# Attention tasks handled in pairs, one pair of sums on another engine, and a new order at the mixer's entry, in one encoder layer on one Trainium2 core

## The chip, the cores and the metric

The program runs on one core of one Trainium2 chip. A core has TensorE (PE, the matrix engine; PEld is its loading of weights), VectorE (DVE), ScalarE (ACT), GpSimd (POOL) and SyncE (SP), each with a queue of its own that it works off in order, and semaphores between them. The metric is the device time of one execution in microseconds, as the median of three runs.

## What is computed

One layer of a streaming encoder for 512 prompt tokens and 32 sample tokens (T = 544), D = 1024, everything in float32:

```
r += 0.5 * post_ffn1(SwiGLU_1(pre_ffn1(r)))             # up1 and down1, D_FF = 2816
z  = pre_mix(r) @ w_in                                   # q | k | v | b | c | xv
     heads A: 8 query heads, 2 key/value heads; a query chunk of 64 sees its own chunk and the two before it;
              a learned sink logit in each softmax's denominator
     heads B: b * causal_depthwise_conv3(c * xv)
r += post_mix(concat(norm_A(A), norm_B(B)) @ w_out)
r += 0.5 * post_ffn2(SwiGLU_2(pre_ffn2(r)))             # up2 and down2
r += post_ple(sigmoid(pre_ple(r) @ w_ple_gate) * (p @ w_ple_proj))
```

All norms are RMS norms over the features. The layer also returns the newest keys, values and convolution rows.

## The kernel before

Activations lie with features on the partitions and tokens along the row; the 544 tokens are two halves of 272, A and B. Each float32 operand of a large product is split into a high part (ScalarE, a copy with rounding, "hi") and a low part (VectorE, the difference, "lo"), and a product is three matmuls: high by high, high by low, low by high. A *unit* is one 128 x 272 result in one of four PSUM banks (`bank`); unit n uses bank n mod 4, so PE may start a unit only when the result four units before it has been read out (*evacuated*). The other four PSUM banks are `misc`.

**Start.** PE turns (transposes) the tokens' tiles `x_tok` into `misc` and `bank`; ACT and DVE copy them to `r`, split the first weights and inputs, and PE begins the units of up1, each as a pass over the high parts (L1846, `hi_pass`) and one over the low ones (L1854, `lo_pass`).

**up1, up2.** After ten single units come seventeen *jobs* (`jobs`, `seven`): a 2x2 block product by seven products of 12 matmuls (Strassen's scheme), L1924 to L1927. A job needs sums of weight blocks: `first_sums` (DVE, L1310) makes two of them in `s31`; `weight_sums` (POOL, L659 and L661) makes two more in `s24`, the second from the first; then ACT makes the high parts (`block_hi`, L774) and DVE the low ones (`block_lo`, L1316) in four pieces per job, in `even_blocks` or `odd_blocks`. ACT copies partial results out of the banks (`kept`, L782 to L796), and DVE adds them. The first job's parts are made while PE is busy with single units, the second job's while it is busy with the first.

**Mixer entry.** down1's last results give two sums of squares over half B: one to scale `y_down`'s half B, one for `r`'s half A (its inverse, `rpre` A, scales the first units' results). PE adds the squares over the partitions (`all_sums`, L1819), ACT takes the root, DVE the inverse (`invert`, L1224). `chain_r` on DVE then updates the residual half B in eight steps (L1232 scale, L1239 add), and the places after single steps at which the units 0 to 3 (k, v, q0, q1 of half A) are evacuated are given in its table. PE needs those evacuations and ACT's high parts of the new residual for units 4 to 7.

**Mixer.** 36 units (`MIX_UNITS`, v = 0 to 35), and 17 attention *tasks* (16 of 64 queries by two heads' groups, one for the sample). Behind unit v = 10 + d PE does the scores of task d (`scores`, L2059), the transposes of task d-1's probabilities (`turn_probs`, L2005) and the weighing of the values for task d-2 (`weigh`, L2084 to L2093); ACT does the exponentials and copies the transposed probabilities, DVE the maxima, the scaling and the copying of the outputs. I call the block of these small matmuls behind a unit a *visit*. DVE's loop over v evacuates unit v, then takes the maxima of task d, then the low parts of a weight (`split_lo`), the output of task d-2 and the scaling of task d. The last rows of the convolution are turned on PE behind unit 33 (`conv_rows`).

The order on every engine is that of the code; nothing is planned at run time.

## Time and profile before

| | |
|---|---|
| median of three runs | 1059.75 us (1059.62 to 1059.94) |
| the profiled execution | 1059.61 us, of which its span 1057.8 us |
| PE busy | 1034.4 us, 98% of the span |
| DVE, ACT, POOL busy | 697.1, 511.3, 277.0 us |
| mean granted TensorE clock | 0.995 |

Busy time of PE is that of pipelined matmuls: one lasts 0.29 us by its record, and in a full stream one starts every 0.12 to 0.125 us. What PE loses is therefore read from the distance between the starts of its instructions, and from the idle times that the profile puts down to a releaser. Times of a row are in microseconds from the span's start.

### The profile page before, as it was taken

The page shows a single profiled execution, that of the slowest core. Times are in us where ns is not written, and L with a number is a line of the kernel's source. Part 1 is how long each engine was busy: PE and PEld are TensorE (multiplying, and loading weights), DVE is VectorE, ACT ScalarE, POOL GpSimd, SP SyncE. Part 2 cuts the span into 40 slices and gives each one's busy share as a digit, 9 for nine tenths or more (in the row PEclk, how much of TensorE's full clock was granted, in tenths as well). Part 3 has the DMA queues.
Part 4 walks back from the last instruction along what each step waited for, and adds up shares of the span by engine and source line. Part 5 has one row for each costly group of instructions (what it writes and reads, how often), then busy time and mean ns, then how long its engine had stood idle before and what let it go on. Part 6 is the DMA issues. An engine that isn't in the chain of part 4 may idle for free.

```text
span 1057.8 us, 20089 instructions
## 1 busy us (share of the span) xinstructions
PE 1034.4 (98%) x8095; PEld 1014.5 (96%) x8095; DVE 697.1 (66%) x1051; ACT 511.3 (48%) x925; POOL 277.0 (26%) x212
## 2 busy tenths in 40 slices
PE   7999999999999999999999999999999999999997
PEld 6999999999999998888999999999999999999897
DVE  5889777777512269677695898987777741127843
ACT  5555555555522354434455555555555642126664
POOL 3114443431111142000323201443434011114221
PEclk8999999999999999999999999999999999999999
DMA  8214343435323303230234121442423532332102
GB/s 246 83 41 111 93 117 84 117 82 143 106 81 110 79 7 80 80 87 21 73 109 120 41 80 41 121 120 81 121 80 108 138 112 73 90 100 84 39 1 85
DMA packets 182678, 94.76 MB, mean 90 GB/s; under 512 B 11768, under 2 KB 180928, under 8 KB 182592
## 3 DMA queue, kind: packets, MB, share of 16 engines
q1 hardware_dynamic: 182576, 93.56, 32.0%
q8 instruction: 60, 0.98, 0.4%
q14 instruction: 26, 0.21, 0.1%
q10 hardware_dynamic: 16, 0.00, 0.0%
HBM read 91.15 MB, written 2.50 MB: 89 GB/s over the span
## 4 chain that ended last, share of the span: by engine, by line
PE 85%; DVE 9%; POOL 2%; ACT 2%; issue 1%; DMA 1%; SPq 0%; POOLq 0%; DVEq 0%; ACTq 0%
PE bank L1797 14%; PE bank L1799 14%; PE bank L1798 14%; PE bank L1924 9%; PE bank L1927 9%; PE bank L1926 9%; PE bank L1846 6%; PE bank L1854 2%; PE misc L2005 2%; PE misc L1924 1%; PE misc L1927 1%; PE misc L1926 1%; DVE w_split L1218 1%; DVE x_lo L1248 1%; DMA raw_up<-w_ffn_gate_up 1%
## 5 line engine op out<-in xcount | busy, mean ns | idle before, releaser
L1799 PE MATMUL bank<-h_hi,w_split 128*128 128x272 f32 x704 | 204.0, 290 | 0.0
L1797 PE MATMUL bank<-h_hi,w_split 128*128 128x272 f32 x704 | 203.0, 288 | 0.0
L1798 PE MATMUL bank<-h_lo,w_split 128*128 128x272 f32 x704 | 202.2, 287 | 0.0
L1218 DVE TENSOR_TENSOR w_split<-raw,w_split 128x1408 fp32r<-128x1408 f32 (+2 forms) x66 | 98.7, 1507 | 146.4 <-ACT w_split L714 146.4
L629 POOL TENSOR_TENSOR ssq<-ssq,sq 128x272 f32<-128x272 f32 x99 | 96.5, 975 | 221.6 <-ACT sq L719 216.1
L1798 PEld LDWEIGHTS bank<-h_lo,w_split 128*128 128x128 f32 x704 | 132.6, 188 | 0.1
L1797 PEld LDWEIGHTS bank<-h_hi,w_split 128*128 128x128 f32 x704 | 132.4, 188 | 0.1
L1799 PEld LDWEIGHTS bank<-h_hi,w_split 128*128 128x128 f32 x704 | 132.3, 188 | 0.0
L1924 PE MATMUL bank<-t_hi,even_blocks 128*128 128x272 f32 x432 | 125.3, 290 | 0.2
L1927 PE MATMUL bank<-t_hi,even_blocks 128*128 128x272 f32 x432 | 125.0, 289 | 0.0
L1926 PE MATMUL bank<-t_lo,even_blocks 128*128 128x272 f32 x432 | 124.4, 288 | 0.0
L659 POOL TENSOR_TENSOR s_rest<-s,raw_up 128x512 f32<-128x512 f32 x32 | 70.6, 2206 | 199.6 <-DVE s L1310 199.6
L714 ACT ACTIVATE w_split<-raw 128x1408 fp32r<-128x1408 f32 (+2 forms) x66 | 81.1, 1240 | 83.0 <-PE bank L1799 76.6
L1924 PE MATMUL bank<-t_hi,odd_blocks 128*128 128x272 f32 x384 | 111.5, 290 | 2.0 <-ACT kept L789 1.1
L1927 PE MATMUL bank<-t_hi,odd_blocks 128*128 128x272 f32 x384 | 111.1, 289 | 0.0
L1926 PE MATMUL bank<-t_lo,odd_blocks 128*128 128x272 f32 x384 | 110.5, 288 | 0.0
L1798 PE MATMUL bank<-x_lo,w_split 128*128 128x272 f32 x320 | 92.1, 288 | 0.0
L1924 PEld LDWEIGHTS bank<-t_hi,even_blocks 128*128 128x128 f32 x432 | 81.3, 188 | 0.6 <-issue 0.6
L1926 PEld LDWEIGHTS bank<-t_lo,even_blocks 128*128 128x128 f32 x432 | 81.4, 188 | 0.0
L1927 PEld LDWEIGHTS bank<-t_hi,even_blocks 128*128 128x128 f32 x432 | 81.3, 188 | 0.0
L1924 PEld LDWEIGHTS bank<-t_hi,odd_blocks 128*128 128x128 f32 x384 | 72.2, 188 | 2.7 <-issue 1.5
L1926 PEld LDWEIGHTS bank<-t_lo,odd_blocks 128*128 128x128 f32 x384 | 72.4, 189 | 0.0
(276 smaller groups left out, 2632.6 us busy)
## 6 DMA issues: line engine op xcount, KB each, us to landing
raw_up<-w_ffn_gate_up SPq DMA_DIRECT2D x88, 512.0 KB, 5.1
raw<-w_ffn_down SPq DMA_DIRECT2D x32, 704.0 KB, 4.9
raw<-w_in SPq DMA_DIRECT2D x14, 512.0 KB, 4.0
raw<-w_ple_gate SPq DMA_DIRECT2D x8, 512.0 KB, 3.7
x_tok<-x_prompt SPq DMA_DIRECT2D x4, 512.0 KB, 5.3
raw<-w_in SPq DMA_DIRECT2D x8, 256.0 KB, 3.8
raw<-w_out SPq DMA_DIRECT2D x16, 128.0 KB, 3.2
raw<-w_out SPq DMA_DIRECT2D x8, 256.0 KB, 3.4
```

The costliest lines, as they stand in the source:

```text
L629: nc.gpsimd.tensor_tensor(dst, dst, sq[:, s % 2, :], ALU.add).then_inc(summed, 1)
L659: nc.gpsimd.tensor_tensor(s24(j)[:, 0, :], s31[:, 1, :], a[:, 0, :], ALU.add).then_inc(s24_made[n], 1)
L714: nc.scalar.activation(chunk_part(c, 0), chunk_raw(c), ACT.Copy).then_inc(hi_made, 1)
L1218: nc.vector.tensor_tensor(chunk_part(c, 1), chunk_raw(c), chunk_part(c, 0).bitcast(F32), ALU.subtract).then_inc(lo_made, 1)
L1797: nc.tensor.matmul(psum(u), wh, hi, start=(k == 0), stop=False)
L1798: nc.tensor.matmul(psum(u), wh, lo, start=False, stop=False)
L1799: mm = nc.tensor.matmul(psum(u), wl, hi, start=False, stop=(k == n - 1))
L1846: nc.tensor.matmul(psum(u), chunk_part(c, part)[:, k, :], high(k, h), start=(k == 0 and part == 0), stop=False)
L1854: mm = nc.tensor.matmul(psum(u), chunk_part(c, 0)[:, k, :], low(k, h), start=False, stop=(k == KD - 1))
L1924: nc.tensor.matmul(out, hi[:, k, :], x_h, start=(k == 0 and p in (1, 2, 7)), stop=False, skip_group_check=True)
L1926: nc.tensor.matmul(out, hi[:, k, :], x_l, start=False, stop=False, skip_group_check=True)
L1927: mm = nc.tensor.matmul(out, lo[:, k, :], x_h, start=False, stop=(k == 3), skip_group_check=True)
```

## The change

It has five parts.

1. **Attention in pairs.** Tasks 2n and 2n+1 are handled together behind unit 10 + 2n (`tasks_of`): scores of the pair, weighing for the pair two visits back, then transposes for the pair one visit back. Nothing is done behind the odd units, except the last task's weighing behind unit 29. Scores, transposed probabilities and outputs of even and odd tasks get places of their own in `misc`. DVE takes the outputs and the maxima *before* it evacuates the unit, and does the scalings after it.
2. **Second job's sums by VectorE.** For job 1 of up1 and of up2, the two sums that POOL made are made by DVE (`second_sums`), ahead of the job's first low parts.
3. **Mixer entry.** `rpre` A is inverted first, then the scale of `y_down` B; units 0 to 3 are evacuated after steps 0, 1, 3 and 4 instead of 2, 3, 5 and 5. The last sum of squares of this entry is issued inside the first low pass instead of ahead of it, and the transposes of the values wait for unit 5's evacuation instead of unit 7's.
4. **Idle transposes at the start.** 4, 8 and 8 transposes of `ones` into an unused bank are put ahead of the gains, ahead of the tokens' tiles and behind the tokens' third tile.
5. **Convolution rows.** They are turned behind unit 34 instead of 33; three groups of squares on ACT move with the tasks.

```diff
-    SUM_HALF = [A, B] + [A, B, A, B] + [A, A, B, B] + ...
-    SUMMED = [8, 16, 30, 40, 38, 48, ...
+    SUM_HALF = [A, B] + [A, A, B, B] + [A, A, B, B] + ...
+    SUMMED = [8, 16, 30, 38, 40, 48, ...
...
+        def tasks_of(v, step):
+            n, other = divmod(v - MIX_ATTN0, 2)
+            first = 2 * (n - step)
+            if step == 2 and first + 1 >= NTASK - 2:
+                return range(NTASK - 1, NTASK) if other and first == NTASK - 3 else \
+                    range(first, first + 2) if not other and first == NTASK - 3 else ()
+            return range(first, min(first + 2, NTASK)) if first >= 0 and not other else ()
+        def behind_pair(d):
+            return min(d - d % 2 + 2, NTASK)
...
             def weight_sums(n, s):
                 for j in range(NJ):
+                    if j == 1:
+                        continue
...
+            def second_sums(n, s, j):
+                a = job_raw(s, j)
+                dve.wait_ge(s31_made[n], j + 1)
+                dve.wait_ge(s24_made[n], 2 * j)
+                nc.vector.tensor_tensor(s24(j)[:, 0, :], s31[:, 1, :], a[:, 0, :], ALU.add).then_inc(s24_made[n], 1)
+                dve.wait_ge(s24_made[n], 2 * j + 1)
+                nc.vector.tensor_tensor(s24(j)[:, 1, :], s24(j)[:, 0, :], a[:, 1, :], ALU.add).then_inc(s24_made[n], 1)
...
                         first_sums(n, s, j + 1)
+                    if not j:
+                        second_sums(n, s, j + 1)
+                    if more:
                         block_lo(n, s, j + 1, 0)
...
             def attention_out(d):
-                dve.wait_ge(pv_done, d + 1)
+                dve.wait_ge(pv_done, behind_pair(d))
+                dve.wait_ge(probs_turned, behind_pair(min(d + 2, NTASK - 1)))
...
-            chain_r(1, B, y_down, SUM0["down1"] + 1, {1: lambda: invert(SUM0["down1"] + 2, rpre[:, A, :]),
-                                                      2: lambda: evacuate(0), 3: lambda: evacuate(1),
-                                                      5: lambda: (evacuate(2), evacuate(3))})
+            invert(SUM0["down1"] + 1, rpre[:, A, :])
+            chain_r(1, B, y_down, SUM0["down1"] + 2, {0: lambda: evacuate(0), 1: lambda: evacuate(1),
+                                                      3: lambda: evacuate(2), 4: lambda: evacuate(3)})
...
             for v in range(4, len(MIX_UNITS)):
+                if v >= MIX_ATTN0:
+                    for d in tasks_of(v - 1, 2):
+                        attention_out(d)
+                    for d in tasks_of(v, 0):
+                        softmax_max(d)
                 evacuate(v)
-                if 0 <= d < NTASK:
-                    softmax_max(d)
...
-                if 2 <= d < NTASK + 2:
-                    attention_out(d - 2)
-                if 0 <= d < NTASK:
-                    softmax_scale(d)
+                if v >= MIX_ATTN0:
+                    for d in tasks_of(v, 0):
+                        softmax_scale(d)
...
+            def idle_turns(n):
+                for _ in range(n):
+                    turn(bank[:, 1, 0:P], ones[:])
             pe.wait_ge(consts, 4)
+            idle_turns(4)
             pe.wait_ge(g_first_in, 16)
             turn(bank[:, 0, 0:KD], g_rows[0:KD, :], KD).then_inc(turned_g, 1)
+            idle_turns(8)
...
             for i in range(XT - 2):
                 turn_x(i)
+            idle_turns(8)
...
             def scores(d):
-                if d:
-                    pe.wait_ge(exp_made, d)
+                if d > 1:
+                    pe.wait_ge(exp_made, behind_pair(d - 2))
...
-                    pe.wait_ge(z_ready, 8)
+                    pe.wait_ge(z_ready, 6)
...
-                    first_units(units, 1, B, lead=LEAD, between=lambda: all_sums(n0 + 3))
+                    first_units(units, 1, B, lead=LEAD, within=lambda: all_sums(n0 + 3))
...
-                if 0 <= d < NTASK:
-                    scores(d)
-                if 1 <= d <= NTASK:
-                    turn_probs(d - 1)
-                if 2 <= d < NTASK + 2:
-                    weigh(d - 2)
+                if v >= MIX_ATTN0:
+                    for d in tasks_of(v, 0):
+                        scores(d)
+                    for d in tasks_of(v, 2):
+                        weigh(d)
+                    for d in tasks_of(v, 1):
+                        turn_probs(d)
```

PE's rows behind one mixer unit, before (scores `zk,zq`, transposes of `probs`, weighing with `v_mixed` and `v_band`; the rows around them are a unit's products). This stands behind every unit from 10 on:

```order
2725 L1799 MATMUL bank<-x_hi_b,w_split 128x272
2726 L2059 MATMUL misc<-zk,zq 128x192 x2
2727 L2005 MATMUL misc<-ident,probs 128x128 x3
2728 L2084 MATMUL misc<-probs_t,v_mixed 128x128
2729 L2087 MATMUL misc<-probs_t,v_band 64x128 x2
2730 L1797 MATMUL bank<-x_hi_a,w_split 128x272
```

And with the change, behind unit 16; the units 15 and 17 have nothing behind them:

```order
2776 L1837 MATMUL bank<-x_hi_b,w_split 128x272
2777 L2107 MATMUL misc<-zk,zq 128x192 x4
2778 L2132 MATMUL misc<-probs_t,v_mixed 128x128
2779 L2135 MATMUL misc<-probs_t,v_band 64x128 x2
2780 L2132 MATMUL misc<-probs_t,v_mixed 128x128
2781 L2135 MATMUL misc<-probs_t,v_band 64x128 x2
2782 L2045 MATMUL misc<-ident,probs 128x128 x6
2783 L1835 MATMUL bank<-x_hi_a,w_split 128x272
```

The same small matmuls stand there for two tasks, in one block, with the weighing ahead of the transposes.

DVE's rows at the mixer's entry, before (`misc` is the scale of `y_down` B, `rpre` that of the units of half A; `zk` and `zv` are the evacuations of units 0 and 1):

```order
260 L1224 RECIPROCAL misc<-misc 128x272
261 L1232 TENSOR_TENSOR y_down<-misc,y_down 128x272 x2
262 L1239 SCALAR_TENSOR_TENSOR r<-y_down,gT,r 128x272
263 L1232 TENSOR_TENSOR y_down<-misc,y_down 128x272
264 L1239 SCALAR_TENSOR_TENSOR r<-y_down,gT,r 128x272
265 L1224 RECIPROCAL rpre<-misc 128x272
266 L1232 TENSOR_TENSOR y_down<-misc,y_down 128x272
267 L1239 SCALAR_TENSOR_TENSOR r<-y_down,gT,r 128x272
268 L1585 TENSOR_TENSOR zk<-bank,rpre 128x272
269 L1232 TENSOR_TENSOR y_down<-misc,y_down 128x272
270 L1239 SCALAR_TENSOR_TENSOR r<-y_down,gT,r 128x272
271 L1551 TENSOR_TENSOR zv<-bank,rpre 128x272
```

And with the change:

```order
262 L1248 RECIPROCAL rpre<-misc 128x272
263 L1248 RECIPROCAL misc<-misc 128x272
264 L1256 TENSOR_TENSOR y_down<-misc,y_down 128x272 x2
265 L1263 SCALAR_TENSOR_TENSOR r<-y_down,gT,r 128x272
266 L1621 TENSOR_TENSOR zk<-bank,rpre 128x272
267 L1256 TENSOR_TENSOR y_down<-misc,y_down 128x272
268 L1263 SCALAR_TENSOR_TENSOR r<-y_down,gT,r 128x272
269 L1587 TENSOR_TENSOR zv<-bank,rpre 128x272
```

Both inverses stand ahead of the chain, and the first two evacuations follow two steps earlier in it.

DVE's rows in the first job of up1, before (`s` holds the first two sums of job 1, `s_rest` the other two, `odd_blocks` job 1's parts, `t_lo` low parts of the tokens' side):

```order
66 L1310 TENSOR_TENSOR s<-raw_up 128x1024
67 L1316 TENSOR_TENSOR odd_blocks<-raw_up,odd_blocks 128x1024
68 L1328 TENSOR_TENSOR tG<-misc,kept 128x272
69 L1297 TENSOR_TENSOR t_lo<-t_raw,t_hi 128x1088
70 L1316 TENSOR_TENSOR odd_blocks<-s,odd_blocks 128x1024
71 L1316 TENSOR_TENSOR odd_blocks<-s_rest,odd_blocks 128x1024
```

And with the change:

```order
66 L1334 TENSOR_TENSOR s<-raw_up 128x1024
67 L1342 TENSOR_TENSOR s_rest<-s,raw_up 128x512
68 L1344 TENSOR_TENSOR s_rest<-s_rest,raw_up 128x512
69 L1349 TENSOR_TENSOR odd_blocks<-raw_up,odd_blocks 128x1024
70 L1361 TENSOR_TENSOR tG<-misc,kept 128x272
71 L1321 TENSOR_TENSOR t_lo<-t_raw,t_hi 128x1088
```

Two additions of 512 columns come in behind `s`, and everything after them stands two places later.

## Rows read from the trace of the kernel before

**Rows 1.** The page, busy time and share of the span

```profile
PE 1034.4 (98%) x8095; PEld 1014.5 (96%) x8095; DVE 697.1 (66%) x1051; ACT 511.3 (48%) x925; POOL 277.0 (26%) x212
```

**Rows 2.** The page, chain that ended last, by engine

```profile
PE 85%; DVE 9%; POOL 2%; ACT 2%; issue 1%; DMA 1%; SPq 0%; POOLq 0%; DVEq 0%; ACTq 0%
```

**Rows 3.** Who PE waited for: us in total, times, longest

```profile
PE bank L1846 <- ACT x_hi_up L732: 3.4, 1, 3.4
...
PE bank L1924 <- ACT kept L789: 1.1, 2, 0.6
PE misc L2005 <- DVE probs L1634: 1.1, 3, 0.5
...
PE bank L1924 <- ACT kept L782: 0.9, 2, 0.4
...
PE bank L1846 <- DVE zq L1567: 0.6, 1, 0.6
PE bank L1846 <- DVE zv L1551: 0.5, 1, 0.5
...
PE misc L2005 <- DVE conv_rows L1700: 0.3, 1, 0.3
...
PE misc L2005 <- DVE zq L1567: 0.3, 1, 0.3
...
PE misc L2059 <- ACT es L1007: 0.3, 1, 0.3
```

**Rows 4.** Start: PE and DVE in order of time (start, us, engine, line, what)

```profile
4.47 3.67 PE L2005 MATMUL misc<-ident,x_tok 128*128 128x128 f32 x16 [0.96 <-DMA x_tok<-x_prompt]
...
12.71 7.00 PE L1846 MATMUL bank<-x_hi_up,w_up 128*128 128x272 f32 x32 [3.42 <-ACT x_hi_up L732]
...
21.12 4.27 PE L1846 MATMUL bank<-x_hi_up,w_up 128*128 128x272 f32 x32
21.18 1.79 DVE L1218 TENSOR_TENSOR w_up<-raw_up,w_up 128x1024 fp32r<-128x1024 f32 x1
```

**Rows 5.** The stretch 12.0 to 18.8: busy PE, PEld, DVE, ACT, POOL, then PEclk

```profile
12.00:18.80 6.80, 6.09 (x27) 6.09 (x28) 5.69 (x9) 5.68 (x12) 3.95 (x4) 0.50 0.71 163
```

**Rows 6.** First job of up1, DVE and POOL in order of time

```profile
82.30 0.69 DVE L1316 TENSOR_TENSOR even_blocks<-raw_up,even_blocks 128x512 fp32r<-128x512 f32 x1
...
84.20 2.21 POOL L659 TENSOR_TENSOR s_rest<-s,raw_up 128x512 f32<-128x512 f32 x1 [11.83 <-DVE s L1310]
...
85.53 2.04 DVE L1297 TENSOR_TENSOR t_lo<-t_raw,t_hi 128x1088 fp32r<-128x1088 f32 x1
87.49 2.30 DVE L1316 TENSOR_TENSOR odd_blocks<-s,odd_blocks 128x1024 fp32r<-128x1024 f32 x1
89.83 1.22 DVE L1316 TENSOR_TENSOR odd_blocks<-s_rest,odd_blocks 128x1024 fp32r<-128x1024 f32 x1
90.97 1.28 DVE L1297 TENSOR_TENSOR t_lo<-t_raw,t_hi 128x1088 fp32r<-128x1088 f32 x1
```

**Rows 7.** Mixer entry, DVE and PE in order of time

```profile
400.42 1.85 DVE L1224 RECIPROCAL misc<-misc 128x272 f32<-128x272 f32 x1
404.18 1.85 DVE L1224 RECIPROCAL rpre<-misc 128x272 f32<-128x272 f32 x1
409.99 0.90 DVE L1567 TENSOR_TENSOR zq<-bank,rpre 128x256 f32<-128x256 f32 x4
410.54 4.93 PE L1846 MATMUL bank<-x_hi_a,w_split 128*128 128x272 f32 x36 [0.59 <-DVE zq L1567]
```

**Rows 8.** One visit, PE in order of time

```profile
450.56 0.29 PE L1799 MATMUL bank<-x_hi_b,w_split 128*128 128x272 f32 x1
450.78 0.59 PE L2059 MATMUL misc<-zk,zq 64*128 64x192 f32 x4
...
452.38 0.40 PE L1797 MATMUL bank<-x_hi_a,w_split 128*128 128x272 f32 x1
452.62 0.29 PE L1798 MATMUL bank<-x_lo,w_split 128*128 128x272 f32 x1
```

More of the change, by code:

```diff
@@ L377, in segments @@
             if c == 0:
-                return [(0, CHUNK, 1, v_band[0:CHUNK, 0])]
+                return [(0, CHUNK, 0, v_band[0:CHUNK, 0])]
             return [(0, P, 0, v_band[:, 0])]
@@ L1001, in softmax_exp @@
                 b, n = d % 2, task_keys(d)
-                act.wait_ge(neg_max, d + 1)
+                act.wait_ge(neg_max, behind_pair(d))
                 for g in range(2):
-                    nc.scalar.activation(probs[:, b, g, 0:n], scores_at[:, g, 0:n], ACT.Exp,
+                    nc.scalar.activation(probs[:, b, g, 0:n], scores_at(d)[:, g, 0:n], ACT.Exp,
                                          bias=nm[:, b, g:g + 1], scale=SCALE, accum_out=rs[:, b, g:g + 1])
@@ L1856, in lo_pass, with first_units @@
                 mm.then_inc(unit_done, 1)
-            def first_units(units, ci, h, hooks_hi={}, hooks_lo={}, second={}, lead=KD, between=lambda: None):
+            def first_units(units, ci, h, hooks_hi={}, hooks_lo={}, second={}, lead=KD, between=lambda: None,
+                            within=lambda: None):
                 def high(k, h):
@@ L1871, in first_units @@
                     lo_pass(u, c, lambda k, h: x_low(ci, k, h), h,
[L1872 removed]
+                            None if n else lambda k: (pe.wait_ge(x_ready, 16 * ci + 8 * h + k + 1),
+                                                      within() if k == KD // 2 else None))
                     if n in hooks_lo:
@@ L2058, in scores @@
                         keys = zk[rows, max(c - 2, 0) * CHUNK:(c + 1) * CHUNK]
-                    mm = nc.tensor.matmul(scores_at[:, g, 0:task_keys(d)], q, keys, start=True, stop=True)
+                    mm = nc.tensor.matmul(scores_at(d)[:, g, 0:task_keys(d)], q, keys, start=True, stop=True)
                 mm.then_inc(scored, 1)
@@ L2068, in turn_probs @@
                     for n in range(3):
-                        tr = turn(bT[:, n * P:(n + 1) * P], both[:, n * P:(n + 1) * P])
+                        tr = turn(turned_probs_at(d, n), both[:, n * P:(n + 1) * P])
                 else:
@@ L2072, in turn_probs @@
                         for g in range(2):
-                            at = (2 * place + g) * P
-                            tr = turn(bT[0:rows, at:at + P], probs[:, d % 2, g, first:first + rows])
+                            tr = turn(turned_probs_at(d, 2 * place + g)[0:rows], probs[:, d % 2, g, first:first + rows])
                 tr.then_inc(turned_p, 1)
             def weigh(d):
-                pe.wait_ge(probs_turned, d + 1)
-                if d:
-                    pe.wait_ge(attn_ready, d)
+                pe.wait_ge(probs_turned, behind_pair(d))
+                if d > 1:
+                    pe.wait_ge(attn_ready, behind_pair(d - 2))
                 if three_chunks(d):
                     c = TASKS[d][0]
-                    nc.tensor.matmul(bO[:, 0:P], v_mixed[:, c - 2, :], probs_t[:, d % 2, 1, :], start=True, stop=False)
+                    nc.tensor.matmul(weighed_at(d), v_mixed[:, c - 2, :], probs_t[:, d % 2, 1, :], start=True, stop=False)
                     for g in range(2):
                         rows = slice(g * DH, (g + 1) * DH)
-                        mm = nc.tensor.matmul(bO[rows, 0:P], v_band[:, c - 2 + g, rows], probs_t[:, d % 2, 2 * g, :],
+                        mm = nc.tensor.matmul(weighed_at(d)[rows], v_band[:, c - 2 + g, rows], probs_t[:, d % 2, 2 * g, :],
                                               start=False, stop=True)
@@ L2092, in weigh @@
                         for g in range(2):
-                            mm = nc.tensor.matmul(bO[g * DH:(g + 1) * DH, 0:P], values[:, g * DH:(g + 1) * DH],
+                            mm = nc.tensor.matmul(weighed_at(d)[g * DH:(g + 1) * DH], values[:, g * DH:(g + 1) * DH],
                                                   probs_t[0:rows, d % 2, 2 * place + g, :],
```

54 lines of the change are left out of this document (28 added, 26 removed).

## Prediction

> **What bounds the kernel.** I read the busy table first: PE is busy for 98% of the span [rows 1]. Then the chain: 85% of it is PE and 9% DVE [rows 2], so the kernel is a stream of matmuls, and only time in which that stream halts or stretches can be won. The list of PE's waits shows where it halts [rows 3]: once for ACT's first high parts at the start (3.4 us), four times for ACT's copies of partial results, two in up1 and two in up2 (1.1 + 0.9), for evacuations at the mixer's entry (0.6 and 0.5, and 0.3 ahead of the values' transposes), for attention (1.1 for scaled probabilities, 0.3 for exponentials) and for the convolution's rows (0.3). These are few microseconds of 1058. The fourth thing to read is the distance of PE's starts, since a matmul that starts late without a recorded wait also costs: PE starts an instruction each 1034.4 / 8095 = 0.128 us on average [rows 1], and 0.12 to 0.125 inside a product.
>
> **The change part by part.**
>
> *Attention, the seams.* In a visit the scores start 0.22 us after the last matmul of the unit, and behind the visit the first product's matmul holds the next one up for 0.24 us [rows 8]. Against 0.125 that is 0.10 to enter and 0.11 to leave. Before, 19 visits (behind units 10 to 28), 17 of them with scores; now 11 (ten even units from 10 to 28, and 29), nine of them with scores. Eight entries and eight exits fewer: 8 x 0.21 = 1.7 us. The small matmuls stay the same in number. Not shown before is the step from weighing one task to weighing the next, which comes seven times; its bounds are nothing and another 0.10, so 1.7 becomes 1.0 at worst. At best the seams inside a visit (scores to transposes, transposes to weighing) halve as well, two of 0.10 for each of 8 pairs, which makes 3.3. I take 1.7, the value of the rows that show a whole seam.
>
> The Trainium skill, TensorEngine Tiling (Array Packing), Key Properties, says that changing the tiling mode drains TensorE. The scores use 64 rows of the array and the weighing with `v_band` 64 columns, and the seam at the scores in the trace fits that. By this rule a pair's visit, which weighs full, halved, full, halved, has nearly as many changes of mode as two single visits, and the part would bring 1.0 instead of 1.7.
>
> *Attention, the waits.* Before, probabilities had to come back from scores, maxima, exponentials and scaling within one unit, some 3 us of product and 1.8 us of visit (450.56 to 452.38 [rows 8]). Now they have two units and a longer visit, about 9.4 us. The 1.1 and 0.3 us of waits [rows 3] should go: 1.4 us. Next in line are the weighing, which waits until DVE has copied the outputs of the pair before, and the evacuations behind the maxima. DVE is busy 66% of its time [rows 1], some 6.2 of the 9.4 us between visits, so about 3 us are idle; the outputs stand behind most of that work, and I take half of the idle time, 1.5 us, as what they come ahead of PE's asking. An evacuated bank is asked for four units later. So I count nothing for either, with the price in a rival below.
>
> *Convolution's rows.* They are asked for a unit later, behind a sum; the wait of 0.3 us [rows 3] goes. DVE is busy there, but has three more microseconds.
>
> *Second job's sums.* In the first job DVE and POOL work side by side and both are slow: POOL's sums take 2.21 us each; under them DVE's `t_lo` takes 2.04 instead of 1.28 and its next part 2.30 instead of 1.22 [rows 6], 1.84 us too much. On DVE the two sums are additions of 128 x 512, nearest row 0.69 us [rows 6]; with a wait between them 1.5 us. DVE thus wins 1.84 - 1.5 = 0.35 us, in rounded terms 0.4, and everything behind it in its queue comes that much earlier. PE's two waits in this stretch name ACT's copies, but ACT's own queue hangs on others: ahead of the first copy on POOL's sums, ahead of the second on DVE, whose low part and addition release the gate's activation. The first wait goes, the second shrinks only by what DVE wins, because DVE's chain sets it; a small new one comes at job 1's first product, since its low part now stands 1.5 us later. What counts for the end is when PE leaves the second wait: 0.4 us earlier, in up1 and in up2: 0.8 us. Bounds: if additions cost 1.22 like those of 1024 columns, DVE loses 0.7 each time (-1.4); if all four waits go, +2.0.
>
> *Mixer entry.* The inverses start at 400.42 and 404.18, 1.85 us each; both orders hold both of them ahead of the evacuations that PE waits for. From 406.06 to 409.99 DVE does four steps of the chain and two evacuations of about 0.45 (0.90 for the two of q0 and q1): (3.93 - 0.9) / 4 = 0.76 us a step [rows 7]. PE resumed at 410.54 with unit 6, and could take unit 7 only after the second q evacuation, at about 410.9. Now that one stands behind five steps instead of six: 0.76 us earlier, and unit 2's 1.2 us earlier still. The first two evacuations come earlier too, and the wait for `zv` (0.5 [rows 3]) goes; but it lay ahead of the wait for q, which ends where DVE lets it, so it is not counted again. The later steps of the residual are no later than before, since the same work precedes them from step 5 on. So 0.8 us. Putting the sum inside the low pass costs 0.5 us of delay to a root that is not waited for. The values' transposes ask for unit 5's evacuation instead of unit 7's: 0.3 us [rows 3]. Together 1.1 us; bounds 0.5 (the first steps of the residual, now behind both inverses and thus 1.9 us later, hold up PE) and 1.7 (all waits of the entry).
>
> *Start.* PE stood still for 3.42 us before 12.71, and from 12.0 to 18.8 the granted clock was 0.50 [rows 4, 5], the 1.2 GHz level: 32 matmuls took 7.00 us, against 4.27 for the 32 at 21.12. The transposes of `ones` fill part of that gap. The eight ahead of the tokens cost 3.67 / 16 = 0.23 us each, 1.8 us, while the tokens were there at 4.47; they delay PE by about 0.8 us, but the first pass at 12.71 hangs on ACT and on a weight's DMA, so I take that as hidden. If the clock then stays at the 2.4 GHz level, PE saves 2.7 us on the first two passes. But the fourth unit's pass needs the low part that DVE ends at 21.18 + 1.79 = 22.97 [rows 4], and PE began it before at about 21.12 + 2.1 = 23.2. DVE's queue has nothing of PE ahead of that. So 0.2 us remain of 2.7; if the clock falls all the same, none.
>
> **Sum.** 1.7 + 1.4 + 0.3 + 0.8 + 1.1 + 0.2 = 5.5 us, against the profiled execution's 1059.6, which makes 1054.1. That execution lies 0.14 under the median of the runs, so 1054.2 is forecast.
>
> **Rivals.**
>
> *The seams stay* (chance 0.17). PE's small matmuls cost what changes of mode cost and not what visits cost, and the sums bring nothing to PE because the new wait at job 1's first product is as long as what was won. Then 1.0 for the seams and 0 for the sums: 4.0 us, 1055.7. The scores' seam speaks for it; the seam behind a visit against it.
>
> *More than the waits* (0.13). All waits in up1, up2 and at the entry go, and the seams inside the visits halve: up to 3.3 + 1.4 + 0.3 + 2.0 + 1.7 + 0.2 = 8.9, of which I would expect some 7.5: 1052.2.
>
> *A hole in the start* (0.07). At the full level PE ends its third pass at about 12.71 + 4.2 + 1.7 + 2.1 = 20.7 and stands still to 22.97, 2.3 us. If the clock falls there, as it did in the longer gap before 12.71, a stretch like that of rows 5 follows: 6.8 us at half, 3.4 lost, now with nothing to hide it: 1057.5.
>
> *Outputs hold the weighing* (0.07), the slower side. `attention_out` now also waits until ACT has copied the next pair's transposed probabilities, and stands behind two maxima, an evacuation with the convolution's steps, perhaps a weight's low part and two scalings. If it comes later than my slack of 1.5 us, PE waits in each of the eight pairs' visits. It must be 0.7 us late on average (8 x 0.7 = 5.6) to eat the whole gain; at 1.0 us late, 1059.7 - 5.5 + 8 = 1062.2. DVE is busy 66% overall [rows 1], which speaks against it.
>
> *The plain forecast* has 0.56, with its own range 1053.0 to 1055.5.
>
> **Numbers.** The range 1051.8 to 1057.3 takes in the first two rivals and the bounds of the seams and sums, and leaves out the hole's upper part and the slower side. A measurement of this kernel tells differences from about 0.2% (2.1 us) on. Faster by more, under 1057.6: the forecast, both rivals near it and nearly all of the hole, 0.87. Within 0.2%: rests of the hole and of outputs a little late, 0.07. Slower: 0.06.
>
> **What would show it.** In the profile after: PE's waits for `probs`, `es` and `conv_rows` gone; visits only behind every second unit, and a distance of 0.24 us to leave one; in up1 DVE's `t_lo` at 1.28 and the next part at 1.22 us, PE's wait for the second copy still there but about 0.4 us shorter in effect; at the entry one wait for an evacuation, ended some 0.8 us earlier against down1's end; at the start no stretch at half the clock, but a wait of PE for a low part of DVE. The forecast is wrong if PE waits for `ac` copies in the visits, if a second stretch at half the clock shows up, or if seams inside the pairs' visits are longer than 0.1 us each.

## The result, and the profile after

| | before | changed |
|---|---|---|
| median of four runs | 1059.68 us (1059.60 to 1059.94) | 1053.43 us (1052.92 to 1053.87) |
| ratio of the two, 95% interval | | 0.9941 (0.993 to 0.9953) |
| span of the profiled execution | 1057.8 us | 1051.1 us |

The kernel became 6.25 us faster. The forecast was 1054.2, its range 1051.8 to 1057.3. The profiled execution of the changed kernel is the fastest of its four, so the two profiled spans differ by 6.7 us, a little more than the medians. The time is right; what follows shows that several of its terms are not, the largest by a factor of two, and that a part of the gain is given back in a place of which the prediction says nothing.

The page, busy time, answers to [rows 1]:

```profile
PE 1032.0 (98%) x8115; PEld 1015.1 (97%) x8115; DVE 696.1 (66%) x1055; ACT 509.5 (48%) x931; POOL 266.0 (25%) x208
```

PE does 20 instructions more (the idle transposes) and is as full as before. Who PE waited for, answering to [rows 3] (us in total, times, longest):

```profile
PE bank L1884 <- ACT x_hi_up L758: 3.1, 1, 3.1
...
PE bank L1884 <- DVE w_up L1242: 0.9, 1, 0.9
PE bank L1964 <- ACT kept L815: 0.8, 2, 0.4
...
PE bank L1884 <- DVE zq L1603: 0.7, 1, 0.7
PE bank L1835 <- DVE w_split L1242: 0.6, 1, 0.6
PE bank L1964 <- DVE tU L1367: 0.5, 1, 0.5
```

The waits for `probs`, `es`, `conv_rows` and `zv` are gone, and so are those of 0.9 us for the copies `kept` of the jobs; the other two for such copies, L789 in [rows 3] and L815 here, are 0.8 us instead of 1.1. New are those for `w_up` at the start, for `w_split` at the end of the mixer's entry, and for `tU` in up2's last job.

To see where the 6.7 us of span went, I cut both traces at the same PE instructions and took the length of each stretch. The table has beside them the kernels of two experiments (below), since it is what they were made for.

| stretch of PE, us | before | changed | `pairs_alone` | `old_sums` |
|---|---|---|---|---|
| start of the span to up1's first job | 78.99 | 78.75 | 78.83 | 79.60 |
| up1's jobs, to down1's first product | 181.87 | 181.34 | 181.84 | 181.86 |
| down1, to the mixer's first product | 133.15 | 133.17 | 133.17 | 133.16 |
| mixer entry, to the first scores | 39.69 | 38.90 | 39.65 | 38.90 |
| first scores to the mixer's first sum of squares | 90.70 | 85.36 | 85.34 | 85.37 |
| that sum (`ssm`) to up2's first job | 132.48 | 132.88 | 132.92 | 132.87 |
| up2's first job to PE's last pair of transposes | 393.73 | 393.52 | 393.71 | 393.75 |
| sum | 1050.61 | 1043.92 | 1045.46 | 1045.51 |

Stretches that an edit does not touch agree to 0.05 us between kernels in the middle rows, to 0.10 in the row from `ssm` on and to 0.07 in the last, so differences of one to two tenths can be read here, which the medians cannot tell. Only the first stretch varies much by itself (78.2 to 79.6 over all kernels), with the landing of the tokens: PE turns the third tile of `x_tok` from 7.0 us on in the kernel with 78.2 (`singles_order`) and from 8.1 on in the one with 79.6 (`old_sums`).

Attention gave 5.34 us where 3.4 were forecast. The piece behind it gave 0.40 back.

### The profile page after: what moved, and what is told of

Read it like the earlier page. It is cut to its first block, busy times and chain, and to the rows that moved or that the text cites. A ratio compares the mean times of both kernels' runs of the same rounds, so it can differ in the third digit from the quotient of the medians.

```text
span 1051.1 us, 20152 instructions
## 1 busy us (share of the span) xinstructions
PE 1032.0 (98%) x8115; PEld 1015.1 (97%) x8115; DVE 696.1 (66%) x1055; ACT 509.5 (48%) x931; POOL 266.0 (25%) x208
## 4 chain that ended last, share of the span: by engine, by line
PE 85%; DVE 9%; ACT 2%; issue 1%; POOL 1%; DMA 1%; SPq 1%; POOLq 0%; DVEq 0%; ACTq 0%
PE bank L1837 14%; PE bank L1835 14%; PE bank L1836 14%; PE bank L1964 9%; PE bank L1967 9%; PE bank L1966 9%; PE bank L1884 5%; PE bank L1892 2%; PE misc L2045 2%; PE misc L1964 1%; PE misc L1967 1%; PE misc L1966 1%; DVE w_split L1242 1%; DVE x_lo L1272 1%; DVE rpre L1248 1%
## 5 line engine op out<-in xcount | busy, mean ns | idle before, releaser
L685 POOL TENSOR_TENSOR s_rest<-s,raw_up 128x512 f32<-128x512 f32 x30 | 66.2, 2207 | 207.6 <-DVE s L1334 207.6
```

What stands on the lines that cost most here:

```text
L685: nc.gpsimd.tensor_tensor(s24(j)[:, 0, :], s31[:, 1, :], a[:, 0, :], ALU.add).then_inc(s24_made[n], 1)
```

## The experiments

Where the time of an experiment says little, since tenths are in question, its verdict rests on the stretches.

### Pairs alone

The kernel before with parts 1 and 5 only; POOL's sums, the entry and the start as before.

> The kernel before with the attention tasks in pairs (and the convolution's rows a unit later) as the only change. Theory 1, read from the two traces: visits and the stretches between them became 5.4 us shorter (3.2 inside the visits, 2.1 around them), and 0.4 of it is given back in the output projection; this part alone gives about 5.0 us, 1054.7. Theory 2, the prediction's own sum: 1.7 for seams, 1.4 and 0.3 for waits, 3.4 in all, 1056.3, and the rest of the gain came from the other parts together. Theory 3: the parts don't add up, and alone it gives under 3 us.

Measured: 1054.43 us (1054.08 to 1055.20), ratio 0.9954 (0.9937 to 0.997). The stretches stand in the table: 5.36 us won in attention, 0.44 given back behind it, nothing elsewhere. Theory 1; the pairs are most of the change, and the parts add up.

### What a change of form costs

Two kernels with the same pairs, the same places and the same waits, only with another order of the small matmuls in a visit. The first:

```diff
-                    for d in tasks_of(v, 0):
-                        scores(d)
-                    for d in tasks_of(v, 2):
-                        weigh(d)
-                    for d in tasks_of(v, 1):
-                        turn_probs(d)
+                    for i in range(2):
+                        for step, work in ((0, scores), (2, weigh), (1, turn_probs)):
+                            ...
+                            for d in tuple(tasks_of(v, step))[i:i + 1]:
+                                work(d)
```

> The changed kernel with the same pairs and the same waits, but inside a visit one task's scores, weighing and turning come first and then the other's, as in two single visits. Theory 1: each change from one kind of small matmul to another costs about 0.10 us. A full pair's visit has 5 such changes, this order 7, so visits grow by 0.2 us each, 1.5 us over eight or nine visits: 1055.0. Theory 2: only the change between the long product and the small matmuls costs, inside a visit the kinds follow each other free: no change, 1053.4.

The second, with `weigh` cut into two parts:

```diff
-                    for d in tasks_of(v, 2):
-                        weigh(d)
+                    both = tuple(tasks_of(v, 2))
+                    if len(both) == 2 and all(three_chunks(d) for d in both):
+                        weigh(both[0], 0), weigh(both[1], 0)
+                        weigh(both[0], 1), weigh(both[1], 1)
+                    else:
+                        for d in both:
+                            weigh(d)
```

Part 0 of `weigh` is the matmul with `v_mixed`, part 1 those with `v_band`.

> The changed kernel, but a pair's two full-width weighings stand together and then its eight 64-column ones, where both tasks have three chunks. Theory 1, 0.10 us for each change of kind: 5 changes become 3 in the six or seven visits of this form, 0.2 us each, 1.2 to 1.4 us faster: 1052.1. Theory 2, the rule that only a change of tiling mode drains: the same two changes fall away, so the same sign, and the size tells what one costs. Theory 3, the changes are free: 1053.4, visits as long as before.

Measured: `singles_order` 1055.31 us (1054.72 to 1055.81), ratio 0.9961 (0.9947 to 0.9975); `modes_grouped` 1050.80 us (1050.42 to 1051.60), ratio 0.992 (0.9903 to 0.9936). One full visit of each, PE in order of time (start, us, then line, what is written and read, and the form: rows of the array by columns). The changed kernel:

```profile
454.86 0.92 PE L2107 MATMUL misc<-zk,zq 64*128 64x192 f32 x8
455.71 0.49 PE L2132 MATMUL misc<-probs_t,v_mixed 128*128 128x128 f32 x2
456.13 0.44 PE L2135 MATMUL misc<-probs_t,v_band 128*64 128x128 f32 x4
456.50 0.49 PE L2132 MATMUL misc<-probs_t,v_mixed 128*128 128x128 f32 x2
456.92 0.44 PE L2135 MATMUL misc<-probs_t,v_band 128*64 128x128 f32 x4
457.29 0.88 PE L2045 MATMUL misc<-ident,probs 128*128 128x128 f32 x6
457.92 0.37 PE L1835 MATMUL bank<-x_hi_a,w_split 128*128 128x272 f32 x1
```

`singles_order`:

```profile
455.02 0.59 PE L2107 MATMUL misc<-zk,zq 64*128 64x192 f32 x4
455.55 0.49 PE L2132 MATMUL misc<-probs_t,v_mixed 128*128 128x128 f32 x2
455.96 0.44 PE L2135 MATMUL misc<-probs_t,v_band 128*64 128x128 f32 x4
456.33 0.55 PE L2045 MATMUL misc<-ident,probs 128*128 128x128 f32 x3
456.81 0.60 PE L2107 MATMUL misc<-zk,zq 64*128 64x192 f32 x4
457.33 0.49 PE L2132 MATMUL misc<-probs_t,v_mixed 128*128 128x128 f32 x2
457.75 0.44 PE L2135 MATMUL misc<-probs_t,v_band 128*64 128x128 f32 x4
458.12 0.55 PE L2045 MATMUL misc<-ident,probs 128*128 128x128 f32 x3
458.43 0.37 PE L1835 MATMUL bank<-x_hi_a,w_split 128*128 128x272 f32 x1
```

`modes_grouped`:

```profile
454.71 0.92 PE L2107 MATMUL misc<-zk,zq 64*128 64x192 f32 x8
455.56 0.71 PE L2133 MATMUL misc<-probs_t,v_mixed 128*128 128x128 f32 x4
456.21 0.66 PE L2139 MATMUL misc<-probs_t,v_band 128*64 128x128 f32 x8
456.79 0.88 PE L2045 MATMUL misc<-ident,probs 128*128 128x128 f32 x6
457.42 0.37 PE L1835 MATMUL bank<-x_hi_a,w_split 128*128 128x272 f32 x1
```

The same 26 matmuls take 3.06, 3.41 and 2.71 us. The reader should look at the form and count how often it changes, the products on both sides (`128*128`) included: 6, 8 and 4 times. Two changes are 0.35 us.

Two things have to be known for the count over all of attention. A row that says `v_band 64*64 x8` can hold four matmuls of 64x64 and four of 128x64, with a change between them: from its start to the next row it takes 0.74 us, where eight of one form take 0.58 (456.21 to 456.79 above). And transposes of 64 or 32 columns count as the full form: in the changed kernel two transposes with 64 columns and two with 128 take 0.38 us together (439.89 to 440.27), about 0.10 each, and the first with 128 starts 0.11 us after the last with 64, as within one form. From the first scores to the first sum of squares, then:

| kernel | changes of form | stretch, us |
|---|---|---|
| before | 69 | 90.70 |
| `singles_order` | 63 | 87.76 |
| changed | 49 | 85.36 |
| `modes_grouped` | 37 | 83.32 |

14 changes cost 2.40 us and 12 cost 2.04: 0.17 us each, in both. Of the two expectations the sign came (theory 1 in both, and in the second theory 2 as well); the 0.10 us for a change was too small.

Between the changed kernel and before there are 20. At 0.17 they are 3.4 us, and 1.9 us of the 5.34 are left. PE's waits in this stretch before, the four of [rows 3] for `probs` and `es` and a fifth of 0.05 us, are 1.4 us of idle time. Read from the distance of starts they cost 1.7, since the matmul behind a wait starts up to 0.08 us later than the idle time says (scores to transposes, for instance, take 0.91, 0.87 and 1.10 us where PE waits and 0.53 where it doesn't). So the changes gave some 3.6 us and the waits 1.7. That makes 0.18 for each of these 20 changes; more of them than in the two experiments lie at the edge of a product, where by my estimate from the distances of starts a change costs 0.19 to enter and 0.21 to leave, against 0.14 to 0.20 inside a visit.

Is it the form that costs, or only that another kind of matmul follows? The steps that keep the form tell. Before, a visit ran scores, transposes, `v_mixed`, `v_band`: transposes and `v_mixed` have the same form, so two visits have 8 changes of form, but 10 of kind. A pair's visit has 6 and 7. Two full visits before took 2 x 1.60 us (450.78 to 452.38 in [rows 8]), a pair's takes 3.06, and the stretches of product between them are 0.20 us longer than their matmuls by 0.125, once for each visit: 3.60 against 3.26. The 0.34 us are two changes at 0.17, as the forms say, and not three. The Trainium skill, TensorEngine Tiling (Array Packing), Key Properties, says that a change of tiling mode drains TensorE: the trace agrees, and the runs give its price, 0.17 us. No kernel here changes the kind and keeps the form and nothing else, but single steps in the traces do. Before, where `v_mixed` follows transposes:

```profile
451.31 0.55 PE L2005 MATMUL misc<-ident,probs 128*128 128x128 f32 x3
451.69 0.39 PE L2084 MATMUL misc<-probs_t,v_mixed 128*128 128x128 f32 x2
452.01 0.44 PE L2087 MATMUL misc<-probs_t,v_band 128*64 128x128 f32 x4
```

and in the changed kernel, where it follows the product:

```profile
508.62 0.38 PE L2132 MATMUL misc<-probs_t,v_mixed 128*128 128x128 f32 x2
508.93 0.44 PE L2135 MATMUL misc<-probs_t,v_band 128*64 128x128 f32 x4
```

From the first `v_mixed` to the first `v_band` it is 0.32 and 0.31 us here, and 0.42 where `v_mixed` follows scores or `v_band` (455.71 and 456.50 above). So a step to another kind in the same form costs nothing that the trace shows, and it is the form that costs.

### Without the idle transposes

```diff
-            idle_turns(4)
...
-            idle_turns(8)
...
-            idle_turns(8)
```

> The changed kernel without the transposes of ones at the start. Theory 1: they kept the clock at its upper level for longer, so without them the stretch at half grows again from 3.4 to some 6.8 us and the fourth unit's pass starts 0.35 us later: 1053.8. Theory 2: the half-level stretch stays at 3.4 us and they bought nothing: 1053.4. Theory 3: they delay the first tokens' transposes, and without them the start is earlier by up to 0.5 us: 1052.9.

Measured: 1053.00 us (1052.47 to 1053.42), ratio 0.9939 (0.9922 to 0.9956), and up1's first job at 78.67 against 78.75. The stretch at half grew to 6.8 us, as theory 1 had it, but nothing was lost by it, as in theory 2: the idle transposes bring nothing. PE in order of time at the start, without them:

```profile
12.39 7.01 PE L1884 MATMUL bank<-x_hi_up,w_up 128*128 128x272 f32 x32 [3.25 <-ACT x_hi_up L758]
...
20.81 4.27 PE L1884 MATMUL bank<-x_hi_up,w_up 128*128 128x272 f32 x32
24.92 0.62 PE L1857 MATMUL misc<-ssq,ones 128*128 128x272 f32 x2
```

and the changed kernel:

```profile
12.50 5.82 PE L1884 MATMUL bank<-x_hi_up,w_up 128*128 128x272 f32 x32 [3.07 <-ACT x_hi_up L758]
...
19.73 2.27 PE L1884 MATMUL bank<-x_hi_up,w_up 128*128 128x272 f32 x16
22.86 2.27 PE L1884 MATMUL bank<-x_hi_up,w_up 128*128 128x272 f32 x16 [0.86 <-DVE w_up L1242]
24.97 0.62 PE L1857 MATMUL misc<-ssq,ones 128*128 128x272 f32 x2
```

The first 32 matmuls take 5.82 instead of 7.01 us, and PE then stands until VectorE has the fourth chunk's low part; the sum of squares follows at the same time. How long the clock stayed at its lower level varied from kernel to kernel with the same transposes: in the profiled executions of seven kernels with 20 of them the stretch at 0.50 lasted nothing, nothing, 3.4 (four times) and 6.8 us, in three kernels without them 3.4, 6.8 and 6.8 us. So it is a tendency, and one that the low part hides. The 0.24 us by which the changed kernel's start is shorter than before lies inside what this stretch varies by itself, and is not shown to be the transposes' doing.

### VectorE's order at the start, and longer filling

```diff
-            chain_lo(0, A, range(4, KD))
             split_lo(3)
+            chain_lo(0, A, range(4, KD))
```

> The changed kernel, but VectorE makes the fourth chunk's low part ahead of the last four low parts of x at the start, not behind them. Theory 1: PE's wait of 0.9 us for this low part, the limit of the start, goes, and the low pass (24.97 now) starts at about 24.1 if the clock is at half for 3.4 us: 0.8 us faster, 1052.6. Theory 2: GpSimd's sum of squares or the tokens' last copies are late next, under 0.3 us. Theory 3: the clock falls for 6.8 us as in the kernel without idle transposes, and nothing is won.

Measured: 1053.05 us (1052.59 to 1053.32), ratio 0.994 (0.9923 to 0.9957). The clock was at half for 6.8 us here; PE's first pass began at 12.86 and took 6.95, and the wait for `w_up` was gone without PE being earlier: theory 3. The second kernel takes `idle_turns(32)` for the last `idle_turns(8)` as well.

> As the run before, and the last row of idle transposes is 32 long instead of 8, so that they fill the gap up to the first product. Theory 1: with PE at work until 12 us the clock does not fall, the first passes take 1.7 us less than with 3.4 us at half, and the start is bound by GpSimd's squares at 23.4: low pass from about 23.6, 0.5 us more won than in the run before, 1052.1. Theory 2: the clock falls anyway; as the run before. Theory 3: the transposes run past the first high part and delay it; slower than the run before.

Measured: 1052.63 us (1052.34 to 1052.77), ratio 0.9937 (0.992 to 0.9954). PE in order of time, and under it the stretch 5.8 to 25 with PEclk in the third place from the end:

```profile
8.81 3.66 PE L2045 MATMUL bank<-ident,ones 128*128 128x128 f32 x32
12.38 4.77 PE L1884 MATMUL bank<-x_hi_up,w_up 128*128 128x272 f32 x32
...
18.57 4.27 PE L1884 MATMUL bank<-x_hi_up,w_up 128*128 128x272 f32 x32
23.86 0.73 PE L1857 MATMUL misc<-ssq,ones 128*128 128x272 f32 x2 [1.03 <-DVE r L1570]
```

```profile
5.80:25.00 19.20, 18.17 (x140) 17.16 (x139) 14.96 (x21) 12.16 (x23) 7.57 (x9) 1.00 0.91 238
```

With no idle time of PE ahead of the first product the clock stayed at its upper level, and it did so in the two other kernels with 32 transposes, where PE stood for 0.5 and 0.3 us there. Two of the seven kernels with 20 transposes kept it too, so three kernels make it likely and don't prove it. The sum of squares is asked 1.1 us earlier. But PE now waits for the tokens' last copy (`r`), and once more behind it for `tG`; at up1's first job 0.3 us are left of the 1.1 (78.43 against 78.75, and 78.47 and 78.42 in the two others). That this much is the edit's doing is not shown, since `singles_order` has 78.21 without it. Theory 1 by its mechanism; its bound was a different one.

### POOL's sums again

```diff
                 for j in range(NJ):
-                    if j == 1:
-                        continue
...
-                    if not j:
-                        second_sums(n, s, j + 1)
```

> The changed kernel with the second job's sums on GpSimd again. Theory 1, from the traces: in up1 and again in up2 the other order won 0.42 to 0.44 us at the second wait for a kept copy; of up2's gain 0.35 us was given back at a wait for tU at the end of the jobs, which the sums on DVE brought. So without them the kernel is 0.5 us slower, 1053.9, and that wait of 0.45 us is gone. Theory 2: the wait for tU has nothing to do with the sums and stays; 0.85 us slower, 1054.3. Theory 3, the prediction's rival: the sums brought nothing, 1053.4.

Measured: 1054.18 us (1053.57 to 1054.50), ratio 0.995 (0.9933 to 0.9967). In the table up1's jobs are 0.52 us longer than in the changed kernel and the last stretch 0.23. Its waits of PE:

```profile
PE bank L1960 <- ACT kept L813: 1.1, 2, 0.6
PE bank L1960 <- ACT kept L806: 0.9, 2, 0.4
```

Both pairs of waits for `kept` are there, and that for `tU` is not. Followed instruction by instruction, PE leaves the second copy's wait 0.52 us earlier with the sums on VectorE in up1 and 0.45 in up2; in up2 0.35 of it are lost again by the new wait, and 0.12 come back later, at a sum of squares at 970 us. Theory 1 by the wait for `tU`, which is gone; the size, 0.75 instead of 0.5, lies as near to theory 2. Theory 3 is out. What links the sums to the wait, some 160 us apart, I don't know: VectorE's `h_raw` in the last job starts 0.35 us later behind the same predecessor, for which the profile names nothing but that predecessor.

### The sum ahead of the low pass

```diff
-                    first_units(units, 1, B, lead=LEAD, within=lambda: all_sums(n0 + 3))
+                    first_units(units, 1, B, lead=LEAD, between=lambda: all_sums(n0 + 3))
```

> The changed kernel with the last sum of squares of down1 asked ahead of the low pass again, not half way into its first unit. Theory 1: the root, its inverse, unit 4's evacuation and the low part of w_split hang on that sum, and unit 8 waits 0.61 us for this low part; the sum 0.5 us earlier makes unit 8 0.5 us earlier and PE's wait 0.1: 1052.9. Theory 2: the root is not waited for, as the prediction had it; then unit 8 starts as before: 1053.4. Theory 3: the sum asks for squares that GpSimd has not added up, PE waits for them up to 0.5 us: 1053.9.

Measured: 1052.73 us (1051.93 to 1053.20), ratio 0.9937 (0.9921 to 0.9954). The mixer entry shrinks from 38.90 to 38.42 us. All engines in order of time, the changed kernel:

```profile
416.31 0.62 PE L1857 MATMUL misc<-ssq,ones 128*128 128x272 f32 x2
416.56 3.87 PE L1892 MATMUL bank<-x_lo,w_split 128*128 128x272 f32 x28
416.96 0.46 ACT L753 ACTIVATE misc<-misc,eps 128x272 f32<-128x272 f32 x1 [4.27 <-PE misc L1857]
417.46 1.86 DVE L1248 RECIPROCAL rpre<-misc 128x272 f32<-128x272 f32 x1 [1.10 <-ACT misc L753]
...
419.77 1.22 DVE L1242 TENSOR_TENSOR w_split<-raw,w_split 128x1024 fp32r<-128x1024 f32 x1
...
421.04 0.39 PE L1835 MATMUL bank<-x_hi_a,w_split 128*128 128x272 f32 x1 [0.61 <-DVE w_split L1242]
```

The last row is unit 8. From the sum to it there is no gap of more than 0.05 us in the chain: root, inverse, evacuation, low part. In `sum_between`, whose entry began 0.26 us later, ScalarE's root starts at 416.74 all the same and unit 8 at 420.82, with no wait recorded. Theory 1: this root is waited for.

### Additions beside VectorE

```diff
-                add(SQ0["mix"] + j, ssm[:, n, :], k == 0)
+                if 2 * KA < j < 3 * KA:
+                    add(SQ0["mix"] + j, ssm[:, n, 0:1], False, n=1)
+                else:
+                    add(SQ0["mix"] + j, ssm[:, n, :], k == 0)
```

> The changed kernel, but GpSimd's three additions of the squares of the attention's second half take in one column instead of 272 (that sum of squares is wrong then: a part of the computation is left out). In every kernel with pairs the stretch from the first sum of the mixer's outputs to up2's first job is 0.40 to 0.44 us longer than before. Theory 1: these additions now run beside a VectorE pair of cinp, which takes 1.11 instead of 0.51 us, VectorE's chain is late by 0.6 us from there on up to the low part that the output projection waits for, and with short additions the 0.4 us come back. Theory 2: the convolution's rows or ScalarE's order give it back; the stretch stays at 132.9 us.

Measured: 1052.58 us in one run; the stretch from the first `ssm` sum to up2's first job is 132.27 us, 0.61 less than in the changed kernel. VectorE and GpSimd there, the changed kernel:

```profile
519.78 2.62 POOL L653 TENSOR_TENSOR ssm<-ssm,sq 128x272 f32<-128x272 f32 x3
521.18 0.44 DVE L1609 TENSOR_TENSOR tG<-bank,rpre 128x272 f32<-128x272 f32 x1 [1.82 <-PE bank L1837]
521.66 1.11 DVE L1627 TENSOR_TENSOR cinp<-cinp,tG 128x240 f32<-128x240 f32 x2
```

and with the short additions:

```profile
520.49 0.53 POOL L653 TENSOR_TENSOR ssm<-ssm,sq 128x1 f32<-128x1 f32 x2 [0.27 <-ACT sq L748]
521.43 0.44 DVE L1612 TENSOR_TENSOR tG<-bank,rpre 128x272 f32<-128x272 f32 x1 [1.82 <-PE bank L1840]
521.91 0.51 DVE L1630 TENSOR_TENSOR cinp<-cinp,tG 128x240 f32<-128x240 f32 x2
```

The pair of `cinp` takes 0.51 instead of 1.11 us when GpSimd is not adding. Theory 1. Of the 0.61 us, 0.33 come at the mixer's second sum of squares, which in the changed kernel PE asks for before VectorE's next output has been squared and added up, and 0.28 at the low part for the output projection, PE's wait for which falls from 0.24 to 0.02 us.

Before, the same additions ran from 523.95 to 528.17, beside two low parts of `w_split`, of 1.79 and 1.38 us, and then VectorE stood idle for 0.53 us until PE gave it the next unit: the delay was hidden. Counted from unit 31's start on PE (524.66 before, 517.78 now) they ended after 3.5 us, and now after 4.6, while the pair of `cinp` begins after 3.9 us in both. Behind it VectorE has hardly a pause until the low part for which PE's output projection waits. The Trainium skill, GPSIMD Engine Reference, 1. Specifications, says that GpSimd's interface is shared with VectorE and that VectorE instructions with two SBUF inputs contend: the trace agrees, since `cinp`, with two such inputs, is slowed. `tG`, which reads one of its two from a PSUM bank, takes 0.44 us with and without the additions, but only 0.29 us of it lie beside one.

### All together

`modes_grouped`, `sum_between` and `low_first_turns` in one kernel.

> The changed kernel with the grouped weighings, the last sum of down1 ahead of the low pass, the fourth low part ahead of the last four of x, and 32 idle transposes. If the gains add up: 2.04 for the weighings, 0.48 at the mixer's entry, 0.3 at the start, from 1053.2 to about 1050.4 us. If the start's gain is only the tokens' landing, 1050.7. If the parts hinder each other, not below the 1050.8 of the grouped weighings alone.

Measured: 1050.01 us (1049.93 to 1050.11), ratio 0.9909 (0.9892 to 0.9925). The last PE instruction stands 2.85 us earlier than in the changed kernel: 2.05 from the weighings, 0.53 at the entry, 0.28 at the start. The first two add up; the third lies inside the variation of the start. One more edit on top puts two of the four squares in question ahead of ScalarE's high part:

```diff
+                if v == 30:
+                    mix_squares(2 * KA, 2 * KA + 2)
                 if v % 8 >= 4 and v < 32:
                     split_hi(c0 + SLOTS + 4 * (v // 8) + v % 4)
...
-                    mix_squares(2 * KA, 3 * KA)
+                    mix_squares(2 * KA + 2, 3 * KA)
```

> The kernel with all of these edits together, and two of the four squares of the attention's second half ahead of ScalarE's high part of w_split instead of behind it, so that GpSimd's additions end before VectorE's pair of cinp begins. If the contention with GpSimd is what gives back 0.4 to 0.6 us ahead of the output projection, the stretch from the mixer's first sum of outputs to up2's first job falls from 132.9 to 132.3 to 132.5 us and the time to about 1049.5. If GpSimd's additions now slow VectorE's low part instead and this is late, or the high part of the weight is missed, the stretch stays at 132.9 or grows: 1050.0 or more.

Measured: 1049.73 us (1049.53 to 1049.81), ratio 0.9906 (0.989 to 0.9923). The stretch from the `ssm` sum to up2 is 132.59 us against 132.86: 0.27 of the 0.61 us come back, those at the second sum of squares; PE's wait for the low part stays at 0.24 us. The `cinp` pair takes 0.79 us instead of 1.11, because GpSimd's three additions, beside VectorE's low part now, last 3.41 us and still reach into it. This is the fastest kernel of the study, 9.7 us under the one before as measured beside it (1059.39); against `all_together` the medians alone would not carry the difference.

## Why the prediction came out

**Seams: the sign was right, the price and what it hangs on were not.** The step that failed is "Against 0.125 that is 0.10 to enter and 0.11 to leave ... 8 x 0.21 = 1.7 us". The distances at the edge of a visit show only what a change of form adds beyond the pipelined product; the rest of it hides in the rows of the small matmuls (four scores take 0.53 us and eight 0.85, so 0.21 of the 0.53 are not the scores'). By changes of form it is 20 x 0.17 = 3.4 us, or 3.6 by the distances. "At best the seams inside a visit ... halve as well ... 3.3" was the nearest of the three, and was kept as a bound only. What costs is the change of form, as the first rival said, and not the visit. The rule on tiling modes, on which I wrote that "the part would bring 1.0 instead of 1.7", was right; my count under it was wrong, since scores, transposes and weighings in a pair's visit have 6 changes where two visits had 8, and visits without `v_mixed` have 4 where two had 8. By the prediction's own sign, seams inside a visit longer than 0.1 us each, this term was wrong.

**Attention's waits: they went, and were worth a little more.** 1.4 us forecast from the idle times, some 1.7 measured by the distances of starts. The rival in which outputs hold the weighing did not come: the outputs of a pair are copied by 452.98 and asked for at 455.71, 2.7 us of slack where I had taken 1.5.

**Convolution's rows: the wait went, nothing was left of it.** "DVE is busy there, but has three more microseconds" looked at this one wait. The stretch became 0.40 us longer instead of 0.3 shorter, by the contention with GpSimd that the shorter attention moved onto VectorE's tight stretch. With the short additions the stretch is 0.21 us shorter than before, about what the wait for the rows was worth. No rival had it.

**Second job's sums: 0.8 forecast, 0.73 measured**, but not in equal halves: 0.52 in up1 and 0.21 in up2, where the wait for `tU` took most of a gain of 0.45, which the prediction did not have. `t_lo` takes 1.28 and the next part 1.22 us, as forecast, and the new small wait at job 1's first product came (0.34 us from start to start).

**Mixer entry: 1.1 forecast, 0.79 measured.** The step that failed is "Putting the sum inside the low pass costs 0.5 us of delay to a root that is not waited for". It is waited for, and costs 0.48; with the sum ahead of the pass the entry gives 1.27. The other steps held: PE is 0.76 us earlier behind the evacuations (0.8 forecast), loses 0.50 at unit 8, and is 0.51 earlier at the transposes of the values (0.3 forecast).

**Start: the limit was right, the gain was none.** VectorE's low part ends at 22.81 (22.97 before) and sets the end of the start where the clock falls for 3.4 us or not at all; with 6.8 us at half PE comes there by itself only about 0.2 us later (before, and `low_first`). The sign "at the start no stretch at half the clock" did not come: the stretch was there in eight of the ten kernels profiled without long filling, hidden each time.

So the errors are +1.9 for the seams, +0.3 for attention's waits, -0.7 behind attention, -0.3 at the entry, and the rest small: 5.5 forecast, 6.69 measured in the span. That the forecast came within a microsecond is luck in part, since the two kinds of error have opposite signs.

## What to carry to other kernels

Count the changes of form of the small matmuls, not the number of interruptions: put together what has the same rows and columns of the array, and let what shares the products' form stand next to the products. When a stretch gets shorter, look at what another engine does beside the *next* one: an addition on GpSimd that was hidden beside an idle VectorE can move onto a tight one. Before an operation is issued later "because nobody waits", follow its chain to the next matmul, here root, inverse, evacuation and low part, 4.7 us long.

## What the runs showed of the hardware

A change between forms (`128*128`, `64*128`, `128*64`) costs 0.17 us on average, of which only about 0.10 shows as a gap at the edge of a product; transposes of 64 columns (`128*64` by the record) next to full ones pay nothing. GpSimd additions of 128 x 272, 0.76 to 0.78 us alone, took 1.57 us each beside VectorE's subtractions of 128 x 1024 (two of the three before that last 4.22 us together), and such a subtraction then took 1.79 instead of 1.22. TensorE's granted clock fell to half in a start with a gap of 3 us in eight of ten kernels, for 3.4 or for 6.8 us, and in none of the three where PE worked through the gap or stood for at most 0.5 us.
